# A two-block network on one core: five edits to the order of work in the second mixer

## The chip, the core and the metric

The kernel runs on one core of a Trainium2 chip. The metric is device time in microseconds (us) of one execution. TensorE (PE) multiplies and transposes, ScalarE (ACT) applies functions and copies, VectorE (DVE) does element-wise arithmetic, SyncE (SP) issues the DMA of the weight stream, GpSimd (POOL) does a little at the start and the end.

## The reference

256 tokens of width 2048 pass through two blocks, and all of it is fp32.

- Block one: RMS norm, an input projection, a pooling mixer, a sparse attention with three branches, gates, and an output projection, added to x.
- Block two, where the change lies: `h = rmsnorm(x)`, `z = h @ w_in`. z is split into q, k, v and a forget gate of 8 attention heads of 128 (forgetting attention), and into q, k, v, input gate, forget gate and output gate `mo` of 4 cell heads (mLSTM; q and k 128 wide, v 256 wide; two chunks of 128 tokens). Then

```
cell  = sigmoid(mo) * cell
mixed = concat(head_rmsnorm(att), head_rmsnorm(cell))
x     = x + mixed @ w_out
x     = x + peer_ffn(rmsnorm(x))        # 8 heads, 128x128 experts
out   = rmsnorm(x)
```

head_rmsnorm divides each head (128 or 256 wide) by its own root mean square over its elements, plus 1e-6 under the root.

## The kernel before, in words

**The weight stream.** All weights arrive as 484 slots of 1 MB (128x2048 fp32). For each slot SP loads one of two raw buffers, ACT rounds it to `whi` (L1011, "the rounding"), DVE subtracts to get the rest `wlo` (L1629, "the rest"), and PE multiplies both halves with both halves of the activations, so that fp32 accuracy is kept. Slots alternate between two buffers. ACT may round slot n+2 when PE has finished slot n (`slot_used`), PE may start slot n when its rest is there (`raw_free`). Each engine works through its own program in the order written; semaphores are the only link between engines. No planner is in play, the order is by hand.

**The second mixer.** Beside the stream slots of the projection, numbered 0 to 23 here (list `MIX`: 8 of `in2_m`, then 16 of `in2_n`, in groups of four, each group filling banks 0 and 1 of PSUM), the attention and the cell are computed in small units. Units of attention u = 0 to 15 stand beside slots 2 to 17; units of the cell u = 0 to 7 stand beside numbers 18 to 25, of which 24 and 25 have no slot: there PE turns (transposes) the mixed activations for the output projection instead.

- On PE a unit turns its probabilities, makes the scores of the unit after the next, runs its slot, and then multiplies probabilities with values (`m_values`). The cell's first four units also make the state.
- On ACT a unit rounds slot n+1 (`mix_split(n+1)`), evacuates the banks if slot n-1 closed a group (`mix_evac(n-1)`: L1305, L1308, or for the last two groups, the output gate `mo`, two Tanh of half the argument at L1311), copies probabilities (`fox_copy`, `m_copy` L1369) and takes exponentials (`fox_exp`, `m_exps` L1361).
- On DVE a cell unit makes the next unit's mask and maximum and weighs its scores (`m_mask`, `m_weigh`), takes the rest of slot n+1, and normalizes its output (`m_out`, L2067 to L2078).
- PE waits for both banks of a group (`bank_free`) before the first slot of the next: slots 8, 12, 16, 20.

**The head norms.** For the attention heads DVE forms the mean square (L2126) in cell unit 1, ACT takes the root (L1391) in the same unit, DVE inverts it (L2129) and scales the heads (L2132) in units 2 and 3. For the cell, `sigmoid_rest` (L2085) makes the sigmoid of Tanh's output, `gate_cells` (L2091) multiplies with it, ACT squares each head (L1375) and takes the second root (L1404), and DVE scales (L2150, two operations).

**The turning.** The mixed activations are 8 pieces. PE turns a piece (L463, 4 transposes), ACT rounds it into hTh (`high_parts`, L1037), DVE takes its rest (`low_parts`, L1619). Pieces 0 to 3 (attention) are turned in cell units 6 and 7; pieces 4 to 7 (cell) need both operations of L2150 and are turned inside the output projection `out2`.

**The output projection.** Its slots are called output slots 0, 1, 2, ... here; 16 in all (L580). Output slot 0 needs pieces 0 and 1 of hTh and hTl and waits for pieces up to 3; output slot 2 needs pieces 4 and on. The function `mixed` (L896) turns pieces 4 to 7 ahead of output slot 2.

Of the kernel before, what the change touches and what calls it, by code (L numbers as in the profile page):

```python
# [28 lines left out]
ALU = mybir.AluOpType  # L29
# [132 lines left out]
def build_two_blocks(nc, x, stream, cmpw, params, stage1, mixw_in, fnw1, fnw, gates_dram, out):  # L162
# [6 lines left out]
    with ExitStack() as ctx:  # L169
# [32 lines left out]
        def region(a, n):  # L202
            return R[:, a:a + n]
# [92 lines left out]
        roots = st[:, 260:264]  # L296
        scales = st[:, 264:268]
        one = st[:, 300:302]
        weighted = region(0, TB * D).rearrange("p (b d) -> p b d", b=TB)
        unused3 = region(TB * D, TB * D).rearrange("p (j c) -> p j c", j=8)  # L300
        part_sq = st[:, 232:240]
# [150 lines left out]
        def _(pe):  # L452
# [443 lines left out]
            def mixed(i, h, s):  # L896
                if (h, s) == (0, 0):
                    pe.wait_ge(hTl_part, 16 + 4)
                if (h, s) == (0, 2):
                    for f in range(4, 8):  # L900
                        turn_piece(2, f)
                if h == 0 and s >= 2:
                    pe.wait_ge(hTl_part, 16 + 2 * (s + 1))
# [96 lines left out]
        def _(act):  # L1000
# [290 lines left out]
            def mix_split(n):  # L1291

                if n < len(MIX):
                    split(*MIX[n])
                elif n == len(MIX):
                    split("out2", 0, 0)
# [45 lines left out]
            fox_exp(0)  # L1342
            mix_split(MIX_FIRST)
            for u in range(units):
                mix_split(u + MIX_FIRST + 1)
                mix_evac(u + MIX_FIRST - 1)
                fox_copy(u)
                if u + 1 < units:
                    fox_exp(u + 1)
                if u == CONV_UNIT + 8:  # L1350
                    act.wait_ge(conv_done, 8)
                    A(conv, conv, ACT.Silu).then_inc(conv_silu, 1)
                if u >= 2:
                    fox_square(u - 2)
# [26 lines left out]
            fox_square(FH * TB - 1)  # L1381
            for u in range(units):
                n = MIX_FIRST + FH * TB + u
                mix_split(n + 1)
                mix_evac(n - 1)
                if u + 1 < units:
                    m_exps(u + 1)
                m_copy(u)
                if u == 1:
                    act.wait_ge(head_ms, 1)  # L1390
                    A(hrt[:, :, 0:8], hss[:, :, 0:8], ACT.Sqrt).then_inc(head_rt, 1)  # L1391
                if u == 4:
                    cell_square(0, 0)
                    cell_square(0, 1)
                if u == 6:
                    cell_square(1, 0)
                    cell_square(1, 1)
                if u >= 6:
                    high_parts(2, "mixnorm", range(2 * (u - 6), 2 * (u - 6) + 2))
# [161 lines left out]
        @block.gpsimd  # L1561
        def _(pool):
            step = stepper(pool, pool_step)
            bufs = pool_buf
            inv = s1("invcnt").rearrange("p (g t) -> p g t", g=NG)
            nc.gpsimd.memset(one, 1.0).then_inc(one_set, 1)
            pool.wait_ge(stage1_in, 16)
            for b in range(2):
                pool.wait_ge(bank_free[b], B0["in_u"][b] + 2)
            step(nc.gpsimd.memset(region(pool_at, 2 * W), 0.0))  # L1570
            for c in range(2 * NG):
                g, w = c // 2, WINDOWS[c // 2]
                u = pT[:, U0 + c, :]
                step(nc.gpsimd.tensor_copy(bufs[0][:, PAD:], u))
                a, s = 0, 1
                while s < w:

                    step(nc.gpsimd.tensor_tensor(bufs[1 - a][:, PAD:], bufs[a][:, PAD:], bufs[a][:, PAD - s:PAD - s + T],
                                                 ALU.add))
                    a, s = 1 - a, 2 * s  # L1580

                step(nc.gpsimd.tensor_scalar(bufs[1 - a][:, PAD:], bufs[a][:, PAD:], 1.0 / w, None, ALU.mult))
                step(nc.gpsimd.tensor_tensor(bufs[1 - a][:, PAD:PAD + 16], bufs[a][:, PAD:PAD + 16], inv[:, g, :],
                                             ALU.mult))
                nc.gpsimd.tensor_tensor(u, bufs[1 - a][:, PAD:], u, ALU.subtract).then_inc(pooled, 1)
                pool.wait_ge(pooled, c + 1)

            pool.wait_ge(fnw_in, 16)
            for c in range(4):
                cs = slice(c * 512, (c + 1) * 512)  # L1590
                pool.wait_ge(x3_ready, c + 1)
                nc.gpsimd.tensor_tensor(weighted[:, 0, cs], xres[:, 0, cs], raw[0][:, cs], ALU.mult).then_inc(x3_weighted[0], 1)
# [3 lines left out]
        def _(dve):  # L1596
# [368 lines left out]
            def mix_split(n):  # L1965

                if n < len(MIX):
                    split(*MIX[n])
                elif n == len(MIX):
                    split("out2", 0, 0)  # L1970
# [90 lines left out]
            def m_out(u):  # L2061
                c, h = divmod(u, MH)
                a = u % 2
                dve.wait_ge(m_num, u + 1)
                dve.wait_ge(m_sm, u + 1)
                if c == 1:
                    step(V.tensor_scalar(numt[:, a, :], bank[2 + a][:, MV:2 * MV], mst[:, a, 4:5], None, ALU.mult))  # L2067
                    V.scalar_tensor_tensor(out=mst[:, a, 5:6], in0=bank[6 + a][:, P:P + 1], scalar=mst[:, a, 4:5],
                                           in1=mst[:, a, 5:6], op0=ALU.mult, op1=ALU.add)
                    step(V.tensor_tensor(numt[:, a, :], bank[2 + a][:, 0:MV], numt[:, a, :], ALU.add))  # L2070
                else:
                    step(V.tensor_copy(numt[:, a, :], bank[2 + a][:, 0:MV]))

                step(V.tensor_scalar(mst[:, a, 6:7], mst[:, a, 5:6], -1.0, None, ALU.mult))
                step(V.tensor_tensor(mst[:, a, 6:7], mst[:, a, 6:7], mst[:, a, 5:6], ALU.max))
                step(V.tensor_tensor(mst[:, a, 6:7], mst[:, a, 6:7], mst[:, a, 3:4], ALU.max))
                step(V.reciprocal(mst[:, a, 7:8], mst[:, a, 6:7]))
                V.tensor_scalar(scr2[:, c, 1024 + h * MV:1024 + (h + 1) * MV], numt[:, a, :], mst[:, a, 7:8], None,  # L2078
                                ALU.mult).then_inc(m_read, 1)

            def sigmoid_rest(g):

                for b in range(TB):
                    dve.wait_ge(bank_free[b], B0["in2_n"][b] + 3 + g)
                step(V.tensor_scalar(vN2[:, 4 + g], vN2[:, 4 + g], 0.5, 0.5, ALU.mult, ALU.add))  # L2085

            def gate_cells(c, h, n):

                dve.wait_ge(m_read, MH * c + h + n)
                sl = scr2[:, c, 1024 + h * MV:1024 + (h + n) * MV]  # L2090
                V.tensor_tensor(sl, sl, vN2[:, 4 + h // 2, c, h % 2 * MV:(h % 2 + n) * MV], ALU.mult).then_inc(cells, 1)  # L2091

            def m_scaled(h):

# [15 lines left out]
            for u in range(units):  # L2110
                n = MIX_FIRST + FH * TB + u
                mix_evac(n - 1)
                if u + 1 < units:
                    m_mask(u + 1)
                    m_weigh(u + 1)
                if u + 1 < MH:
                    m_scaled(u + 1)
                if u < MH:
                    m_state(u)
                mix_split(n + 1)  # L2120
                if u >= 6:
                    low_parts(2, "mixnorm", range(2 * (u - 6), 2 * (u - 6) + 2))
                m_out(u)
                if u == 1:
                    dve.wait_ge(head_sq, FH * TB)
                    V.tensor_scalar(hss[:, :, 0:8], hss[:, :, 0:8], 1.0 / DH, EPS, ALU.mult, ALU.add).then_inc(head_ms, 1)  # L2126
                if u == 2:
                    dve.wait_ge(head_rt, 1)
                    step(V.reciprocal(hrt[:, :, 0:8], hrt[:, :, 0:8]))  # L2129
                if u in (2, 3):  # L2130
                    fa = scr2[:, u - 2, 0:1024].rearrange("p (h e) -> p h e", h=FH)
                    V.tensor_tensor(fa, fa, bc(hrt[:, u - 2, 0:8].unsqueeze(2), [P, FH, DH]), ALU.mult).then_inc(xn_ready, 1)  # L2132
                if u == 3:
                    sigmoid_rest(0)
                    gate_cells(0, 0, 2)
                if u in (4, 5):
                    gate_cells(1, u - 4, 1)
                if u == 6:
                    sigmoid_rest(1)
                    gate_cells(0, 2, 2)  # L2140
                if u in (6, 7):
                    gate_cells(1, u - 4, 1)

            dve.wait_ge(head_sq, FH * TB + units)
            V.tensor_scalar(hss[:, :, 8:12], hss[:, :, 8:12], 1.0 / MV, EPS, ALU.mult, ALU.add).then_inc(head_ms, 1)
# [346 lines left out]
```

## Time and profile before

| what | value |
|---|---|
| three timed runs | 3084.39, 3084.81, 3084.92 us, median 3084.81 |
| the profiled execution, time | 3083.82 us |
| its span, first to last instruction | 3082.0 us |
| mean granted clock of TensorE | 0.990 |
| busy share of the span | PE 97%, weight loads 87%, DVE 57%, ACT 41%, POOL 1% |
| chain that ended last | PE 83%, DVE 11%, ACT 4% |
| slots 0 to 23 of the second mixer | about 1140 to 1330 us of the span |
| output projection `out2` | from 1344.5 us of the span |

The profile is of one execution. Times in the views are counted from the start of the span. The time in brackets at the end of a row of the timeline is the idle time of that engine just ahead of it, and who ended it. The profiled execution's own time is 1.8 us over its span.

### The profile page before, as it was taken

The page shows a single profiled execution, that of the slowest core. Times are in us where ns is not written, and L with a number is a line of the kernel's source. Part 1 is how long each engine was busy: PE and PEld are TensorE (multiplying, and loading weights), DVE is VectorE, ACT ScalarE, POOL GpSimd, SP SyncE. Part 2 cuts the span into 40 slices and gives each one's busy share as a digit, 9 for nine tenths or more (in the row PEclk, how much of TensorE's full clock was granted, in tenths as well). Part 3 has the DMA queues.
Part 4 walks back from the last instruction along what each step waited for, and adds up shares of the span by engine and source line. Part 5 has one row for each costly group of instructions (what it writes and reads, how often), then busy time and mean ns, then how long its engine had stood idle before and what let it go on. Part 6 is the DMA issues. An engine that isn't in the chain of part 4 may idle for free.

```text
span 3082.0 us, 46953 instructions
## 1 busy us (share of the span) xinstructions
PE 2984.3 (97%) x18947; PEld 2689.7 (87%) x18947; DVE 1750.0 (57%) x2414; ACT 1253.0 (41%) x1491; POOL 44.8 (1%) x62
## 2 busy tenths in 40 slices
PE   8999999999998999889999999999999999999998
PEld 7887899999987888767899999988888999988887
DVE  5555555554555556565589988744445454444444
ACT  4334444544344334444343344444443333334444
POOL 0000022000000000000000000000000000000000
PEclk9999999999999999989999999999999999999999
DMA  5555433335444554334544455455556655545554
GB/s 206 203 202 222 175 139 119 129 137 177 178 174 153 190 184 146 123 107 160 185 163 176 160 171 174 166 189 192 191 195 232 242 186 178 185 178 195 191 191 177
DMA packets 90195, 542.56 MB, mean 176 GB/s; under 512 B 9328, under 2 KB 25840, under 8 KB 26352
## 3 DMA queue, kind: packets, MB, share of 16 engines
q1 hardware_dynamic: 70992, 513.94, 46.8%
q10 hardware_dynamic: 19104, 27.27, 2.5%
q8 instruction: 67, 1.10, 0.1%
q14 instruction: 32, 0.26, 0.0%
HBM read 530.68 MB, written 10.49 MB: 176 GB/s over the span
## 4 chain that ended last, share of the span: by engine, by line
PE 83%; DVE 11%; ACT 4%; issue 1%; DMA 0%; ACTq 0%; DVEq 0%; SPq 0%
PE bank L487 28%; PE bank L961 23%; PE bank L500 9%; PE bank L580 8%; PE bank L504 5%; DVE wlo L1629 4%; PE bank L555 3%; ACT whi L1011 2%; PE bank L753 2%; PE bank L620 1%; DVE R L2255 1%; PE bank L710 1%; DVE hT L1619 1%; DVE R L2250 1%; DVE R L2263 0%
## 5 line engine op out<-in xcount | busy, mean ns | idle before, releaser
L1629 DVE TENSOR_TENSOR wlo<-raw,whi 128x2048 fp32r<-128x2048 f32 (+1 forms) x484 | 1103.7, 2281 | 1135.5 <-ACT whi L1011 1134.2
L1011 ACT ACTIVATE whi<-raw 128x2048 fp32r<-128x2048 f32 (+1 forms) x484 | 920.9, 1903 | 1318.7 <-PE bank L961 411.4
L487 PE MATMUL bank<-hT,whi 128*128 128x256 f32 x6400 | 1192.8, 287 | 6.6 <-DVE wlo L1629 5.0
L487 PEld LDWEIGHTS bank<-hT,whi 128*128 128x128 f32 x6400 | 993.9, 192 | 11.4 <-DVE wlo L1629 5.4
L487 PE MATMUL bank<-hT,wlo 128*128 128x256 f32 x3200 | 904.5, 283 | 0.0
L487 PEld LDWEIGHTS bank<-hT,wlo 128*128 128x128 f32 x3200 | 611.7, 191 | 0.0
L500 PE MATMUL bank<-hT,whi 128*128 128x512 f32 x1280 | 447.7, 399 | 3.0 <-DVE wlo L1629 3.0
L504 PE MATMUL bank<-hT,wlo 128*128 128x256 f32 x1280 | 343.9, 281 | 1.3 <-DVE wlo L1629 1.3
L500 PEld LDWEIGHTS bank<-hT,whi 128*128 128x128 f32 x1280 | 236.2, 188 | 58.5 <-issue 6.6
L961 PE MATMUL bank<-whi,ghi 128*128 128x512 f32 x1016 | 273.3, 391 | 6.1 <-DVE glo L2327 6.1
L961 PE MATMUL bank<-wlo,ghi 128*128 128x512 f32 x1016 | 272.8, 391 | 0.0
L961 PE MATMUL bank<-whi,glo 128*128 128x512 f32 x1016 | 271.7, 389 | 0.0
L580 PE MATMUL bank<-whi,hT 128*128 128x512 f32 x768 | 242.9, 395 | 15.5 <-DVE wlo L1629 9.9
L504 PEld LDWEIGHTS bank<-hT,wlo 128*128 128x128 f32 x1280 | 240.7, 189 | 7.8 <-DVE wlo L1629 1.7
L961 PEld LDWEIGHTS bank<-whi,ghi 128*128 128x128 f32 x1016 | 191.4, 189 | 46.1 <-issue 6.5
L961 PEld LDWEIGHTS bank<-wlo,ghi 128*128 128x128 f32 x1016 | 191.8, 189 | 40.1
L961 PEld LDWEIGHTS bank<-whi,glo 128*128 128x128 f32 x1016 | 190.9, 188 | 39.8
L580 PEld LDWEIGHTS bank<-whi,hT 128*128 128x128 f32 x768 | 146.2, 190 | 50.1 <-issue 18.2
L580 PE MATMUL bank<-wlo,hT 128*128 128x512 f32 x384 | 151.1, 394 | 0.0
L945 PE MATMUL bank<-R 128*128 128x128 f32 x512 | 98.9, 274 | 2.5 <-DVE R L2255 2.2
L555 PE MATMUL bank<-whi,hT 128*128 128x512 f32 x256 | 87.5, 414 | 9.7 <-ACT R L1311 4.9
L580 PEld LDWEIGHTS bank<-wlo,hT 128*128 128x128 f32 x384 | 73.3, 191 | 15.0
(322 smaller groups left out, 1976.5 us busy)
## 6 DMA issues: line engine op xcount, KB each, us to landing
raw<-stream SPq DMA_DIRECT2D x484, 1024.0 KB, 4.8
R<-cmpw ACTq DMA_DIRECT2D x8, 1024.0 KB, 5.6
gates_dram<-R ACTq DMA_DIRECT2D x64, 128.0 KB, 4.7
R<-gates_dram ACTq DMA_DIRECT2D x16, 512.0 KB, 5.1
xres<-x SPq DMA_DIRECT2D x2, 1024.0 KB, 5.9
R<-mixw ACTq DMA_DIRECT2D x1, 1024.0 KB, 6.6
R<-fnw ACTq DMA_DIRECT2D x1, 1024.0 KB, 6.3
raw<-fnw SPq DMA_DIRECT2D x1, 1024.0 KB, 4.7
```

The lines of the kernel that those rows point to most:

```text
L487: last = mm(bank[b][:, t * T:(t + 1) * T], w[t][:, ks], x_[:, k, :], start=(at == 0 and n == 0), stop=(at == KC - 1 and n == 2))
L500: return mm(bank[s][:], whi[t][:, k * P:(k + 1) * P], hT2[:, k, :, :].rearrange("p a t -> p (a t)"), start=(k == 0), stop=(k == KC - 1))
L504: mm(bank[s][:, 0:T], wlo[t][:, k * P:(k + 1) * P], hTh[:, k, :], start=False, stop=False)
L555: last = mm(bank[b][:], x_[:, k, ts_], w[t][:, kk * 512:(kk + 1) * 512], start=(k == 0 and n == 0), stop=(k == KC - 1 and n == 2))
L580: last = mm(bank[2 * h + b][:], x_[:, k, ts_], w[t][:, kk * 512:(kk + 1) * 512], start=(k == 0 and n == 0), stop=(k == KC - 1 and n == 2))
L620: last = mm(bank[6 + v][0:NC4, 0:CH], kb[v][:, l, :], cw[n % 2][:, ll * CH:(ll + 1) * CH], start=(l == 0), stop=(l == CB - 1))
L710: last = mm(o, vN1[:, br, k, kv * DH:(kv + 1) * DH], PT[:, a, j * P:(j + 1) * P], start=False, stop=(j == 2 * nb - 1))
L753: last = mm(bank[s][:, e * T:(e + 1) * T], w[t][:, ks], y[:, k, :], start=(k == 0 and m == 0), stop=(k == 7 and m == 2))
L945: last = mm(bank[4 + (2 * s + q) % 4][:, c * P:(c + 1) * P], second_hot[:, k // 2, :], first_hot[:, k // 2, :], start=True, stop=True)
L961: last = mm(bank[4 * b + c][:], x_[:, t, ts_], w[t][:, c * 512:(c + 1) * 512], start=(first and s == 0 and n == 0), stop=(last_group and s ...
L1011: A(whi[t][:, 0:w], raw[t][:, 0:w], ACT.Copy).then_inc(hi_ready[t], 1)
L1629: V.tensor_tensor(wlo[t][:, 0:w], raw[t][:, 0:w], whi[t][:, 0:w].bitcast(F32), ALU.subtract).then_inc(raw_free[t], 1)
```

## The change

Five edits, all in block two's mixer.

1. ACT: `mix_evac(n-1)` stands ahead of `mix_split(n+1)`, in the attention units and in the cell units.
2. ACT: the root of the attention heads' mean square moves from cell unit 1 to cell unit 0, and a dummy Exp follows it (on two constants of a new pair `back`). DVE forms the mean square in unit 0, between the rest of slot 19 and `m_out(0)`.
3. ACT: in cell units 6 and 7 `m_copy(u)` stands ahead of `m_exps(u+1)`.
4. DVE: `m_out` multiplies with 0.5 in its last operation, and the gate is (Tanh + 1) times that in one operation: `sigmoid_rest`'s operation (two of them, L2085) is gone, its waits stay (`tanh_made`). The gates of heads 2 (both chunks) and 3 (chunk 0) move from the end of unit 6 to unit 7, behind the rests of pieces 2 and 3 and ahead of `m_out(7)`.
5. PE: pieces 4 to 7 are turned ahead of output slot 1 instead of output slot 2.

```diff
+        back = st[:, 302:304]
...
-                if (h, s) == (0, 2):
+                if (h, s) == (0, 1):
                     for f in range(4, 8):
                         turn_piece(2, f)
...
             for u in range(units):
+                mix_evac(u + MIX_FIRST - 1)
                 mix_split(u + MIX_FIRST + 1)
-                mix_evac(u + MIX_FIRST - 1)
                 fox_copy(u)
...
                 n = MIX_FIRST + FH * TB + u
+                mix_evac(n - 1)
                 mix_split(n + 1)
-                mix_evac(n - 1)
+                if u >= units - 2:
+                    m_copy(u)
                 if u + 1 < units:
                     m_exps(u + 1)
-                m_copy(u)
-                if u == 1:
+                if u < units - 2:
+                    m_copy(u)
+                if u == 0:
                     act.wait_ge(head_ms, 1)
                     A(hrt[:, :, 0:8], hss[:, :, 0:8], ACT.Sqrt).then_inc(head_rt, 1)
+                    A(back[:, 1:2], back[:, 0:1], ACT.Exp)
...
-            nc.gpsimd.memset(one, 1.0).then_inc(one_set, 1)
+            nc.gpsimd.memset(st[:, 300:304], 1.0).then_inc(one_set, 1)
...
-                V.tensor_scalar(scr2[:, c, 1024 + h * MV:1024 + (h + 1) * MV], numt[:, a, :], mst[:, a, 7:8], None,
-                                ALU.mult).then_inc(m_read, 1)
+                V.tensor_scalar(scr2[:, c, 1024 + h * MV:1024 + (h + 1) * MV], numt[:, a, :], mst[:, a, 7:8], 0.5,
+                                ALU.mult, ALU.mult).then_inc(m_read, 1)
...
-                step(V.tensor_scalar(vN2[:, 4 + g], vN2[:, 4 + g], 0.5, 0.5, ALU.mult, ALU.add))
...
-                V.tensor_tensor(sl, sl, vN2[:, 4 + h // 2, c, h % 2 * MV:(h % 2 + n) * MV], ALU.mult).then_inc(cells, 1)
+                V.scalar_tensor_tensor(out=sl, in0=vN2[:, 4 + h // 2, c, h % 2 * MV:(h % 2 + n) * MV], scalar=1.0, in1=sl,
+                                       op0=ALU.add, op1=ALU.mult).then_inc(cells, 1)
...
                 mix_split(n + 1)
+                if u == 0:
+                    dve.wait_ge(head_sq, FH * TB)
+                    V.tensor_scalar(hss[:, :, 0:8], hss[:, :, 0:8], 1.0 / DH, EPS, ALU.mult, ALU.add).then_inc(head_ms, 1)
                 if u >= 6:
                     low_parts(2, "mixnorm", range(2 * (u - 6), 2 * (u - 6) + 2))
+                if u == 7:
+                    gate_cells(0, 2, 2)
+                    gate_cells(1, 2, 1)
                 m_out(u)
-                if u == 1:
-                    dve.wait_ge(head_sq, FH * TB)
-                    V.tensor_scalar(hss[:, :, 0:8], hss[:, :, 0:8], 1.0 / DH, EPS, ALU.mult, ALU.add).then_inc(head_ms, 1)
...
                 if u == 3:
-                    sigmoid_rest(0)
+                    tanh_made(0)
                     gate_cells(0, 0, 2)
                 if u in (4, 5):
                     gate_cells(1, u - 4, 1)
                 if u == 6:
-                    sigmoid_rest(1)
-                    gate_cells(0, 2, 2)
-                if u in (6, 7):
-                    gate_cells(1, u - 4, 1)
+                    tanh_made(1)
+                if u == 7:
+                    gate_cells(1, 3, 1)
```

## Rows read from the trace of the kernel before

**Rows 1.** The profile's page, busy time by engine and share of the span.

```profile
PE 2984.3 (97%) x18947; PEld 2689.7 (87%) x18947; DVE 1750.0 (57%) x2414; ACT 1253.0 (41%) x1491; POOL 44.8 (1%) x62
```

**Rows 2.** Windows: stretch, length, busy by engine, clock, DMA share, GB/s.

```profile
1259.00:1310.00 51.00, 43.92 (x175) 34.86 (x176) 23.77 (x67) 19.33 (x36) 0.00 (x0) 0.87 0.29 103
```

**Rows 3.** Waits, 1139 to 1420: engine, line, releaser: us, times, longest.

```profile
PE bank L555 <- ACT R L1311: 4.9, 1, 4.9
...
PE bank L580 <- DVE wlo L1629: 6.9, 2, 6.0
...
PE bank L580 <- DVE hT L1619: 2.4, 1, 2.4
```

**Rows 4.** Timeline of PE: first matmul of slots 8, 12 and 16.

```profile
1200.40 0.47 PE L555 MATMUL bank<-whi,hT 128*128 128x512 f32 x1 [1.40 <-issue]
...
1229.80 0.50 PE L555 MATMUL bank<-whi,hT 128*128 128x512 f32 x1 [1.35 <-ACT R L1308]
...
1259.20 0.50 PE L555 MATMUL bank<-whi,hT 128*128 128x512 f32 x1 [1.99 <-ACT R L1308]
```

**Rows 5.** Chain of waits: start, us, what; slots 15, 16 and 20.

```profile
1251.01 5.66 PE bank L555 x24
...
1259.20 7.37 PE bank L555 x24
...
1301.16 7.19 PE bank L555 x24
```

**Rows 6.** Timeline of ACT, the evacuation ahead of slot 12.

```profile
1229.17 0.58 ACT L1308 ACTIVATE R<-bank 128x512 f32<-128x512 f32 x1
```

**Rows 7.** Timeline of ACT, cell units 1 and 2.

```profile
1287.32 1.91 ACT L1011 ACTIVATE whi<-raw 128x2048 fp32r<-128x2048 f32 x1 [8.12 <-PE bank L555]
...
1291.02 1.28 ACT L1391 ACT_TABLE_LOAD   x1
1296.64 0.22 ACT L1391 ACTIVATE st<-st 128x16 f32<-128x16 f32 x1 [4.34 <-DVE st L2126]
...
1298.68 1.28 ACT L1311 ACT_TABLE_LOAD   x1
1299.97 1.08 ACT L1311 ACTIVATE R<-bank 128x512 f32<-128x512 f32 x2
```

**Rows 8.** Timeline and source line: last table load ahead of block one's Tanh.

```profile
379.04 1.28 ACT L1164 ACT_TABLE_LOAD   x1
...
L1183 ACT ACTIVATE R<-bank,par x32: 448/451/476, 525.3 to 747.3; 128x256 f32<-128x256 f32 x32
```

**Rows 9.** Chain of waits, first and last row of a stretch of DVE.

```profile
1308.81 0.44 DVE R L2072
...
1322.11 2.21 DVE wlo L1629
```

**Rows 10.** Timeline of DVE, end of the cell.

```profile
1340.94 0.69 DVE L2085 TENSOR_SCALAR R<-R 128x1024 f32<-128x1024 f32 x1
1341.66 1.03 DVE L2091 TENSOR_TENSOR R<-R 128x512 f32<-128x512 f32 x2
...
1350.40 2.28 DVE L1629 TENSOR_TENSOR wlo<-raw,whi 128x2048 fp32r<-128x2048 f32 x1
```

**Rows 11.** Timelines of PE, ACT and DVE around output slots 1 to 3.

```profile
1358.33 1.91 PE L463 MATMUL bank<-par,R 128*128 128x128 f32 x16
...
1358.97 3.03 ACT L1037 ACTIVATE hT<-bank,par 128x256 fp32r<-128x256 f32 x8 [9.31 <-PE bank L463]
...
1359.85 3.23 DVE L1619 SCALAR_TENSOR_TENSOR hT<-bank,par,hT 128x256 fp32r<-128x256 f32 x8 [7.16 <-ACT hT L1037]
...
1361.83 3.76 ACT L1011 ACTIVATE whi<-raw 128x2048 fp32r<-128x2048 f32 x2
1373.45 1.92 ACT L1011 ACTIVATE whi<-raw 128x2048 fp32r<-128x2048 f32 x1 [7.86 <-PE bank L580]
1378.89 1.92 ACT L1011 ACTIVATE whi<-raw 128x2048 fp32r<-128x2048 f32 x1 [3.52 <-PE bank L580]
```

More of the change, by code:

```diff
@@ L2077, in m_out, with tanh_made @@
                 step(V.reciprocal(mst[:, a, 7:8], mst[:, a, 6:7]))
-                V.tensor_scalar(scr2[:, c, 1024 + h * MV:1024 + (h + 1) * MV], numt[:, a, :], mst[:, a, 7:8], None,
-                                ALU.mult).then_inc(m_read, 1)
-            def sigmoid_rest(g):
+                V.tensor_scalar(scr2[:, c, 1024 + h * MV:1024 + (h + 1) * MV], numt[:, a, :], mst[:, a, 7:8], 0.5,
+                                ALU.mult, ALU.mult).then_inc(m_read, 1)
+            def tanh_made(g):
                 for b in range(TB):
                     dve.wait_ge(bank_free[b], B0["in2_n"][b] + 3 + g)
-                step(V.tensor_scalar(vN2[:, 4 + g], vN2[:, 4 + g], 0.5, 0.5, ALU.mult, ALU.add))
             def gate_cells(c, h, n):
```

## The prediction

> **What bounds the kernel now.** I read the busy shares first: TensorE is busy 97% of the span [rows 1], so only what PE waits for, or runs at the low clock, can be won. The windows over the second mixer then show where that is: in the stretch of the cell units PE is busy 43.9 of 51 us at a mean granted clock of 0.87 [rows 2], while the whole span has 0.99. Third, the waits of that stretch name three places [rows 3]: PE waits 4.9 us for ScalarE's Tanh ahead of slot 20, up to 6.0 us for VectorE's rest ahead of output slot 2, and 2.4 us for hTl ahead of output slot 0. The timeline adds three small ones, 1.40, 1.35 and 1.99 us ahead of slots 8, 12 and 16 [rows 4]. After the longer ones the next slot is slow: slot 15 took 5.66 us, slots 16 and 20, after gaps, 7.37 and 7.19 [rows 5]; that is the 1.2 GHz level for their first part, 2.4 GHz after. The gaps ahead of slots 8 and 12 have no slow slot behind them.
>
> **Edit 1, evacuation first.** ACT rounds slot n+2 (1.91 us, the operation as in [rows 7]) and only then evacuates for 0.58 us [rows 6]; both wait for the same last matmul. Turned round, the bank is free 0.58 us after the slot, when PE is still in the small matmuls between two slots. At slots 8 and 12 these take longer than 0.58 us, so the idle time goes whole: 1.40 + 1.35. Ahead of slot 16 there are no scores to make (the units end) and some 0.25 us stay: 1.99 − 0.25 = 1.75. Sum 4.5 us. With that gap no larger than the small ones, slot 16 should run at the full clock: 7.37 − 5.66 = 1.7 us more. The price: the rounding comes 0.6 us later at these places. It is hidden, since rounding and rest together take 1.91 + 2.3 us and PE's slot over 5.6 us; probabilities and exponentials behind the pair on ACT keep their time, as the pair's sum is the same.
>
> **Edit 2, the root in unit 0.** Before, ACT loads the root's table at 1291.02, waits for VectorE's mean square until 1296.64 (4.34 us), then rounds slot 21, loads a table for Tanh (1.28) and does two Tanh in 1.08 [rows 7]. All of that stood between slot 19 and slot 20. In unit 0 ACT is idle 8.12 us until the rounding at 1287.32 [rows 7]; the new work there is load 1.28, a wait for DVE's mean square (behind the rest of slot 19, about 1282.5), the root 0.2, load 1.28, the dummy Exp: about 5 us, done near 1284.2, and covered. VectorE's new wait in unit 0 is for squares made some 6 us earlier, and what is queued behind it is `m_out(0)`, which waits for PE until 1287 anyway. So neither costs anything; without the cover each would cost its own length once.
> At unit 2 two Tanh now follow slot 19 directly: 1.08 us, against the about 1.6 us of small matmuls that PE has there. The 4.9 us go whole, and the slow part of slot 20 with them, 7.19 − 5.66 = 1.5. Sum 6.4. Late next is VectorE. From `m_out(2)` at 1308.81 to the rest of slot 23 at 1324.3 the chain is VectorE's alone [rows 9]: 15.5 us for two units, and PE's own work for the same was 16.2, so it just fits; one `sigmoid_rest` operation less (0.69, [rows 10]) makes it 14.8. For slots 21 and 22 I get margins of 2 and 0.6 us in the same way. So the gain is kept up to slot 23.
> That Tanh needs no load behind an Exp is shown in block one: the last load ahead of its Tanhs (525 to 747 us) is an Exp's, at 379.04, and the next is a Silu's at 671 [rows 8]. If it needed one here, 1.28 us come in front, of which PE would feel some 0.8.
>
> **Edit 3, copy first in units 6 and 7.** PE's `m_values(6)` starts earlier, but the chain at the end goes through masks, exponentials and pieces, not through it. What remains is one copy less (about 0.15 us) ahead of the rounding of pieces 0 and 1.
>
> **Edit 4, gates.** Between `m_out(6)` and the rests of pieces 2 and 3 VectorE had 0.69 us of `sigmoid_rest` and 1.03 us of gates [rows 10], 1.67 from start to start. The first is gone, the second stands behind the rests. The rests are ready by then: PE turns piece 2 as soon as the rest of piece 0 exists, as before. Output slot 0 so starts 1.67 + 0.15 = 1.8 us sooner. The end of the cell (roots, L2150) comes sooner only by what is really removed: 0.72 + 0.15 = 0.87. The gate's operation with two steps costs as much as with one (the rests, of the same kind with three operands, take 0.40 each in [rows 11], a gate of the same 256 columns 0.43), and the extra factor 0.5 in `m_out` I take at 0, bounded by 0.1 us in each of eight.
>
> **Edit 5, turning ahead of output slot 1.** Before: VectorE's rest for output slot 1 ends at 1350.40 + 2.28 = 1352.7 [rows 10]; slot 1 runs until 1358.3; then 16 transposes 1.91, ACT's eight parts 3.03 and two roundings 3.76, VectorE's eight parts 3.23 and the rest of slot 2 [rows 11], and PE stands idle for 6.0 us [rows 3]. From start of slot 1 to start of slot 2: 13.5 us. After, counted from the start t of VectorE's rest for slot 1: PE turns from about t + 0.3 (slot 0 ends there, and the last L2150 has just ended) to t + 2.3; the rest is there at t + 2.3; slot 1 runs to t + 8.0. ACT rounds the pieces from t + 0.9 to 3.9, then slot 2 to 5.8. VectorE takes the pieces' rests from t + 2.3 to 5.5 and slot 2's from 5.8 to 8.0. So slot 2 starts at t + 8.1, 5.8 after slot 1. The gain is 13.5 − 5.8 = 7.7, with the 0.87 above 8.6. Three chains meet here within 0.2 us (turns against the rest of slot 1, VectorE against slot 1 itself), so this is the softest term; whichever is late costs its lateness. Output slot 2 also loses its slow part: it ended at 1373.45, 7.15 us after its start at 1366.3, the next took 5.44 [rows 11]: 1.7. From there PE runs without a gap in either case. The stream does not bind: raw buffers are freed some 5.9 us before they are wanted at the tightest place.
>
> **The sum.** 4.5 + 1.7 + 6.4 + 8.6 + 1.7 = 22.9 us, of 3083.82 of the profiled execution: 3060.9. The median of the runs lies 0.99 above that execution, so 3061.9, and I say 3062.0.
>
> **A rule weighed.** The low level follows the gap of 1.99 us but not those of 1.40 and 1.35 [rows 4, 5]. The Trainium skill ("TensorE: Matmul & The Clock Gate", the section on the HAM clock gate) says that the low clock is the default, released by activity, and that the moment of change is not tied to the kernel's work and shifts between runs. By the rows alone three slow parts go (1.7 + 1.5 + 1.7 = 4.9 us); by the rule such parts may turn up at other places. It is the first rival.
>
> **The rivals.**
> - *The clock falls elsewhere.* The gaps close but the three slow parts come back behind the low activity that stays (between attention and cell, and in units 6 and 7). Gain 22.9 − 4.9 = 18: 3067. For it: the mean clock of 0.87 over a stretch with few long gaps [rows 2]. Against: in the rows each slow part stands right behind a gap that goes. 12%.
> - *The turn is given back.* The transposes run at the low clock (1.9 us more, in front of slot 1), or VectorE, with 7.8 us of work in a row and no rest between, holds slot 2 up by 2 to 3 us, which brings back a slow part too. Gain 17 to 19: 3067. For it: three chains within 0.2 us. Against: output slot 0 runs just ahead of the turns for 7 us, the last part at the full clock. 13%.
> - *The tail's gap stays whole*, because something I do not see holds the turns: gain 12.6, 3072. 5%.
> - *Nothing arrives.* A later stage takes the time up. Against it: PE-bound, back to back for some 80 us behind output slot 2. About 3085. 4%.
> - *Slower: PE at the low level for whole slots.* With the turns and the second rounding pressed into output slots 0 and 1 PE waits in short pieces, and the clock does not come back. A slot at 1.2 GHz costs 5.66 us more. From four such slots (22.6) on the whole gain is used up; six give 3096. Against: no slot in the rows is slow for its whole length. 3%.
>
> **How the numbers follow.** My forecast of 3062 has 63%, its own band 3058.5 to 3065.5 (0.1 in each `m_out`, the Tanh's load of 0.8, the soft term). With the first two rivals 88% lie under 3069; I give 3057.5 to 3069.0. Under 0.2% (6 us) a measurement of this kernel would hardly tell a change from none. Faster by more than that: 63 + 12 + 13 + 5 = 93%; within: 4%; slower: 3%.
>
> **What would show it.** The slots 8, 12 and 16 start with under 0.3 us of idle time; slot 20 starts right behind its small matmuls and takes 5.7 us; L1391 has no wait ahead of a rounding, and Tanh no load; output slot 0 starts 14.6 − 1.8 = 12.7 us after slot 23 ends and output slot 2 27.8 us after it (36.3 before). The forecast is wrong if PE has a gap of over 1 us ahead of slot 20 or output slot 2, or if the granted clock over the cell units stays at 0.87 while the gaps are gone.

## The result, and the profile after

| | before | after |
|---|---|---|
| median of the runs | 3084.86 us | 3062.20 us |
| the profiled execution | 3083.82 us | 3062.96 us |
| its span | 3082.0 us | 3061.2 us |
| mean granted clock | 0.990 | 0.992 |
| slot 7's end to slot 23's end | 132.3 us | 118.9 us |
| slot 23's end to output slot 2's end | 43.5 us | 33.5 us |

The ratio is 0.9923 (95% interval 0.9906 to 0.994): 23.8 us faster by the ratio, 22.7 by the medians. The forecast was 3062.0. The two last lines of the table are taken from the timelines (start of the small matmuls behind slots 7 and 23, start of the rounding that waits for output slot 2). They give 13.4 + 10.0 = 23.4 us inside the stretch that was changed. The spans differ by 20.8 only, since slot 7 ended 2.8 us later in the profile after, 1200.4 against 1197.65, in stages that the change does not touch; 2.6 us of it are longer busy time of PE for the same matmuls, so low clock. Behind output slot 2 both profiles take the same time to the end, 1708.6 and 1708.3 us: no later stage took the gain back.

The busy time of PE, on the page of the changed kernel [rows 1]: 5.4 us less over the whole span, at the same number of matmuls.

```profile
PE 2978.9 (97%) x18947; PEld 2686.7 (88%) x18947; DVE 1748.6 (57%) x2412; ACT 1253.5 (41%) x1492; POOL 44.8 (1%) x62
```

Windows over the stretch that was changed, first of the kernel before, then of the changed kernel [rows 2]: slot 7's end to slot 23's end, and slot 23's end to output slot 2's end. The clock is the third column from the end.

```profile
1197.65:1329.96 132.31, 120.59 (x531) 96.29 (x530) 84.73 (x195) 55.42 (x104) 0.00 (x0) 0.95 0.35 124
1329.96:1373.45 43.49, 30.88 (x127) 24.46 (x126) 26.55 (x60) 17.77 (x40) 0.00 (x0) 0.80 0.27 97
```

```profile
1200.44:1319.38 118.94, 116.67 (x532) 93.87 (x531) 84.77 (x194) 55.85 (x105) 0.00 (x0) 0.97 0.39 137
1319.38:1352.87 33.49, 26.94 (x127) 21.33 (x126) 25.38 (x59) 18.01 (x41) 0.00 (x0) 0.95 0.28 96
```

PE is busy for 143.6 us there instead of 151.5, and idle for 8.8 instead of 24.3. So of the 23.4 us some 7.9 are clock and 15.5 idle time. Over the matmuls of the window in [rows 2], from slot 16 to slot 20 (174 of its 175), the clock went from 0.87 to 0.92:

```profile
1257.46:1299.40 41.94, 39.94 (x174) 32.23 (x175) 25.13 (x70) 20.88 (x37) 0.00 (x0) 0.92 0.32 110
```

Waits of PE in the changed kernel, 1139 to 1400 [rows 3]. The three long ones are gone; what is left lies in the tail, between slot 23 and output slot 1, but for 1.43 us of the first line, which stand ahead of slot 18 and stood there before too:

```profile
PE bank L853 <- DVE st L2063: 3.8, 2, 2.4
...
PE bank L464 <- DVE hT L1624: 1.8, 1, 1.8
...
PE bank L464 <- DVE R L2157: 1.3, 1, 1.3
...
PE bank L581 <- DVE hT L1624: 0.8, 1, 0.8
```

First matmul of slot 16 in PE's timeline [rows 4], with 0.28 us of idle time in place of 1.99. Slots 8 and 12 have none at all.

```profile
1257.46 0.47 PE L556 MATMUL bank<-whi,hT 128*128 128x512 f32 x1 [0.28 <-ACT R L1309]
```

Slots 16 and 20 in the chain of waits [rows 5], 5.73 and 5.44 us instead of 7.37 and 7.19. (Without a gap ahead of it the first matmul of slot 20 starts while the small ones still run, and the chain leaves these 0.35 us out: in the timeline the slot lasts from 1292.17 to 1297.96, 5.8 us.)

```profile
1257.46 5.73 PE bank L556 x24
...
1292.52 5.44 PE bank L556 x24
```

ScalarE in cell units 0 to 2 of the changed kernel [rows 7]. Root and both loads stand between 1275.8 and 1280.9, all in its idle time (2.63 us of it are left in front of the rounding). The two Tanh follow slot 19 without a load, and the rounding of slot 21 comes behind them:

```profile
1275.84 1.28 ACT L1395 ACT_TABLE_LOAD   x1
1279.20 0.21 ACT L1395 ACTIVATE st<-st 128x16 f32<-128x16 f32 x1 [2.08 <-DVE st L2128]
1279.43 1.28 ACT L1396 ACT_TABLE_LOAD   x1
1280.73 0.20 ACT L1396 ACTIVATE st<-st 128x1 f32<-128x1 f32 x1
1283.56 1.91 ACT L1012 ACTIVATE whi<-raw 128x2048 fp32r<-128x2048 f32 x1 [2.63 <-PE bank L556]
...
1290.75 1.08 ACT L1312 ACTIVATE R<-bank 128x512 f32<-128x512 f32 x2 [3.51 <-PE bank L556]
1291.72 1.92 ACT L1012 ACTIVATE whi<-raw 128x2048 fp32r<-128x2048 f32 x1
```

The tail on PE: the end of slot 23 (L862), output slot 0, the turning, output slot 1:

```profile
1319.38 0.60 PE L862 MATMUL bank<-R 128*128 128x256 f32 x2
...
1332.09 0.47 PE L581 MATMUL bank<-whi,hT 128*128 128x512 f32 x1 [0.85 <-DVE hT L1624]
...
1339.05 1.97 PE L464 MATMUL bank<-par,R 128*128 128x128 f32 x16 [1.27 <-DVE R L2157]
1341.25 0.50 PE L581 MATMUL bank<-whi,hT 128*128 128x512 f32 x1 [0.23 <-DVE wlo L1634]
```

and on VectorE [rows 10, 11]: the rests of slot 1, of the pieces and of slot 2 follow each other, with 0.28 us between the last two.

```profile
1338.91 2.29 DVE L1634 TENSOR_TENSOR wlo<-raw,whi 128x2048 fp32r<-128x2048 f32 x1
1341.11 3.22 DVE L1624 SCALAR_TENSOR_TENSOR hT<-bank,par,hT 128x256 fp32r<-128x256 f32 x8
1344.61 2.29 DVE L1634 TENSOR_TENSOR wlo<-raw,whi 128x2048 fp32r<-128x2048 f32 x1 [0.28 <-ACT whi L1012]
```

Output slot 2 follows slot 1 without a gap: PE goes on at 1347.0, where slot 1 ends. ScalarE's roundings behind slot 1 and slot 2 show it [rows 11]:

```profile
1347.12 1.92 ACT L1012 ACTIVATE whi<-raw 128x2048 fp32r<-128x2048 f32 x1 [2.55 <-PE bank L581]
1352.87 1.92 ACT L1012 ACTIVATE whi<-raw 128x2048 fp32r<-128x2048 f32 x1 [3.83 <-PE bank L581]
```

### The profile page after: what moved, and what is told of

Same layout as the page of the kernel before. It is cut to its first block, busy times and chain, and to the rows that moved or that the text cites. A ratio compares the mean times of both kernels' runs of the same rounds, so it can differ in the third digit from the quotient of the medians.

```text
span 3061.2 us, 46950 instructions
## 1 busy us (share of the span) xinstructions
PE 2978.9 (97%) x18947; PEld 2686.7 (88%) x18947; DVE 1748.6 (57%) x2412; ACT 1253.5 (41%) x1492; POOL 44.8 (1%) x62
## 4 chain that ended last, share of the span: by engine, by line
PE 84%; DVE 10%; ACT 4%; issue 1%; DMA 0%; ACTq 0%; DVEq 0%; SPq 0%
PE bank L488 29%; PE bank L962 23%; PE bank L501 9%; PE bank L581 8%; PE bank L505 5%; DVE wlo L1634 4%; PE bank L556 3%; ACT whi L1012 2%; PE bank L754 2%; PE bank L621 1%; DVE R L2262 1%; PE bank L711 1%; DVE hT L1624 1%; DVE R L2257 1%; DVE R L2270 0%
```

## The experiments

The theory is the prediction's list of steps, with one addition made for the runs: edits 1 and 2 meet at slot 20 and are not independent there. The rivals are in the expectations. Two measures are given for each run: the ratio to the kernel before with its 95% interval, from repeated runs of both kernels on the same chip; and stretches inside the profile, from which low-clock parts of other stages are kept out. The intervals are 5 to 8 us wide, so single microseconds rest on the stretches alone. "Stretch 1" is slot 7's end to slot 23's end (132.3 us before, 118.9 after), "stretch 2" slot 23's end to output slot 2's end (43.5 and 33.5).

### Edit 1 alone

```diff
-                mix_split(u + MIX_FIRST + 1)
                 mix_evac(u + MIX_FIRST - 1)
+                mix_split(u + MIX_FIRST + 1)
```

and the same for `n` in the cell units.

> Edit 1 alone on the kernel before: the evacuation ahead of the rounding, in the attention and the cell units. Theory A (my steps, which interact at slot 20): slots 8, 12, 16 give 4.5 us, slot 16's slow part 1.7; and at slot 20, with the root still in unit 1, the banks come free after wait, table load and two Tanh, without the rounding of 1.9 us between: 1.9 more. Sum 8.1 us, 3076.7. Theory B (the edits are independent and slot 20 belongs to edit 2): 6.2 us, 3078.6. Theory C (the evacuation only shifts the wait to the later rounding): 0 to 2 us. In the trace: idle ahead of slots 8, 12, 16 under 0.3 us and slot 20 about 3 us behind its small matmuls under A, 4.9 under B.

Ratio 0.9975 (0.9966 to 0.9983), 7.7 us (5.2 to 10.5), which allows A and B and rules out C. The stretch decides: 124.2 us, 8.1 less than before, as A has it. First matmul of slot 20 in this kernel's timeline of PE:

```profile
1294.38 0.47 PE L555 MATMUL bank<-whi,hT 128*128 128x512 f32 x1 [3.08 <-ACT R L1311]
```

3.08 us of idle time instead of 4.88: edit 1 alone takes 1.8 us of a wait that the change's title gives to the root.

### Edit 2 alone

```diff
-                if u == 1:
+                if u == 0:
                     act.wait_ge(head_ms, 1)
                     A(hrt[:, :, 0:8], hss[:, :, 0:8], ACT.Sqrt).then_inc(head_rt, 1)
+                    A(back[:, 1:2], back[:, 0:1], ACT.Exp)
```

with VectorE's mean square moved likewise.

> Edit 2 alone: root of the attention heads in unit 0, dummy Exp behind it, order of rounding and evacuation as before. Theory A: behind slot 19 ScalarE still rounds 1.82 us and then does two Tanh (1.08), the banks are free 2.9 us after the slot, PE's small matmuls take 1.6 to 1.9: 1.3 us of idle time stay of 4.9. Gain 3.6, and the slow part of slot 20 (1.5) goes too, as gaps of 1.4 had none behind them: 5.1 us, 3079.8. Theory B (independent edits): 6.4 us, 3078.4. Theory C (the table loads and the new wait in unit 0 cost what they save): within 1 us of before.

Ratio 0.9989 (0.998 to 0.9998), 3.4 us (0.6 to 6.2). Stretch 1: 128.8, 3.5 less. The idle time ahead of slot 20 is 1.27 us, as A has it, but the slow part of slot 20 stays. PE's timeline of this kernel and its window over slot 20:

```profile
1297.69 0.57 PE L556 MATMUL bank<-whi,hT 128*128 128x512 f32 x1 [1.27 <-ACT R L1312]
```

```profile
1297.70:1304.80 7.10, 7.10 (x24) 5.75 (x25) 3.16 (x6) 0.66 (x3) 0.00 (x0) 0.76 0.40 147
```

The slot took 7.1 us at a mean clock of 0.76, behind a gap shorter than the 1.40 and 1.35 us that slots 8 and 12 had without harm [rows 4]. So A's size of the gap is right and its 1.5 us for the clock is not. The measured 3.5 is the 3.6 of the gap alone. The ratio's interval would allow all of A and the upper end of C; only B lies outside it, and barely. The stretch decides.

### Edits 1 and 2 together

> Edits 1 and 2 together. The steps of the prediction: 4.5 + 1.7 + 6.4 = 12.6 us, 3072.2, with no idle time over 0.3 us ahead of slots 8, 12, 16, 20 and slot 20 in 5.7 us or less. Under theory A of the two single runs the sum of the singles (8.1 + 5.1 = 13.2) is about what both give; the wait at slot 20 is split between them. If the cell units are bound by VectorE once the gap is gone, slots 21 to 23 show waits for its rest and the sum is 2 to 3 us smaller.

Ratio 0.9964 (0.9951 to 0.9977), 11.1 us (7.1 to 15.1). Stretch 1: 119.2 us, 13.1 less. Slots 8, 12 and 20 have no idle time ahead of them, slot 16 has 0.27, and slot 20 takes 5.6 us. The singles sum to 8.1 + 3.5 = 11.6; the rest, 1.5, is the slow part of slot 20, which neither edit removes alone. The third possibility did not occur: of slots 21 to 23 only slot 23 has to wait for VectorE's rest (ready at 1312.26, slot 23 starts at 1312.31), and that by about 0.2 us, as in the kernel before.

### Edit 5 alone

```diff
-                if (h, s) == (0, 2):
+                if (h, s) == (0, 1):
```

> Edit 5 alone: pieces 4 to 7 turned ahead of output slot 1. My steps: in the kernel before output slot 0 ends at 1351.7 and the rest of slot 1 is there at 1352.7, so the turning (1.9 us) ends 0.9 us too late and holds slot 1 by that; gain 7.7 - 0.9 + slow part of output slot 2 (1.7) = 8.5 us, 3076.4. Rival: the turning ahead of slot 1 is only worth it with the gates moved; alone slot 1 is held by 2 us or more and VectorE holds slot 2: gain 5 or less, 3080.

Ratio 0.9979 (0.997 to 0.9988), 6.5 us (3.7 to 9.3). Stretch 2: 35.5 us, 8.0 less than before, against 8.5 expected. The turning starts when output slot 0 ends, at 1351.98, and slot 1 follows it at 1353.6, 23.4 us behind slot 23 where it was 22.8 before (0.9 later was expected, 0.6 it is); slot 2 waits 0.57 us for VectorE. The stretch rules the rival (5 us or less) out; the timing alone would allow it.

### The changed kernel without edit 5

> The changed kernel without edit 5: pieces 4 to 7 turned ahead of output slot 2 again. My steps: output slots 0 and 1 as in the changed kernel (slot 1 starts 11.5 us sooner than before), then 1.9 us of turning and 6.0 us of idle time ahead of slot 2, and its slow part. Slower than the changed kernel by 7.7 + 1.4 = 9.1 us: 3071.3. Rival (the turn is hidden already by the gates moved in edit 4): by under 4 us.

Ratio 0.9971 (0.9959 to 0.9983). Stretch 2: 45.3 us, 11.8 longer than in the changed kernel, where 9.1 was expected. First matmuls of output slots 1 and 2 in its timeline of PE:

```profile
1339.73 0.80 PE L581 MATMUL bank<-whi,hT 128*128 128x512 f32 x1 [3.44 <-DVE wlo L1634]
...
1354.85 0.77 PE L581 MATMUL bank<-whi,hT 128*128 128x512 f32 x1 [6.02 <-DVE wlo L1634]
```

The rival is ruled out. What I had not counted: output slot 0 now ends 3.4 us ahead of slot 1's rest, and without the turning in that time PE idles and runs slot 1 at the low clock too (the turning starts at 1346.9, 7.2 us after slot 1). The turning fills this hole, and that is worth 1.4 us beside its own. A further 1.0 us is clock in output slot 2: it takes 8.3 us here (1354.85 to 1363.16, mean granted clock 0.68), where I had put the 7.2 of the kernel before.

### The changed kernel without edit 4

```diff
+                step(V.tensor_scalar(vN2[:, 4 + g], vN2[:, 4 + g], 0.5, 0.5, ALU.mult, ALU.add))
...
                 if u == 6:
                     tanh_made(1)
+                    gate_cells(0, 2, 2)
+                if u in (6, 7):
+                    gate_cells(1, u - 4, 1)
```

with the gates of unit 7 and the factor 0.5 taken out.

> The changed kernel without edit 4: the sigmoid's operations back, the gates at the end of unit 6, no factor in m_out. Output slot 0 starts 1.7 us later and the chain of the cell ends 0.7 us later. Theory A: output slot 0 runs at the full clock (5.7 us) as in the changed kernel, ends ahead of the turning's release, and only 0.7 us are lost: 3062.9. Theory B: its clock is low again (7.2 us, as in the kernel before and in the runs of edits 1 and 2 alone), it ends after the release and the turning comes behind the rest of slot 1: 1.5 to 2 us lost, 3064.

Ratio 0.9934 (0.9921 to 0.9948). Stretch 2: 35.3 us, 1.8 more, which is B. Output slot 0, the turning, slots 1 and 2 in its timeline of PE:

```profile
1333.99 0.47 PE L581 MATMUL bank<-whi,hT 128*128 128x512 f32 x1 [2.48 <-DVE hT L1624]
...
1341.16 1.91 PE L464 MATMUL bank<-par,R 128*128 128x128 f32 x16
...
1342.83 0.48 PE L581 MATMUL bank<-whi,hT 128*128 128x512 f32 x1
...
1349.11 0.47 PE L581 MATMUL bank<-whi,hT 128*128 128x512 f32 x1 [0.56 <-DVE wlo L1634]
```

Slot 0 starts 14.4 us behind slot 23 (12.7 in the changed kernel), takes 7.2 us and so ends at 1341.16, behind the release of the turning at 1339.95. The turning then holds slot 1, by 0.6 us over its rest, which is ready at 1342.15. The run takes back both halves of edit 4, the removed operation and the moved gates; which of them slot 0's clock hangs on was not run.

### The changed kernel without edit 3

> The changed kernel without edit 3: in units 6 and 7 the copy behind the exponentials again. My step: 0.15 us later at output slots 0, 1 and 2, which no timing shows: 3062.3. Rival: m_values(6) and m_values(7) then come late on PE, in front of output slot 0, and cost the 1 us that they take: 3063.3.

Ratio 0.9925 (0.9912 to 0.9939). Stretch 2: 33.7 us, 0.2 more. `m_values(6)` again has 3.3 us of idle time ahead of it, and nothing that ends the stage waits for it. Output slot 0 starts 12.9 us behind slot 23 where the changed kernel has 12.7 in both of its profiles. The step is right, its size too small for a timing. (This kernel's median lies 2.9 us over the changed kernel's beside it, and its profiled execution as much. Of that, 1.5 us stand ahead of slot 8, which started at 1201.9, and 1.5 us behind output slot 2; the edit touches neither.)

### The changed kernel without the dummy Exp

> The changed kernel without the dummy Exp behind the root. Theory A: the next function that needs the table is the exponential of unit 1, not Tanh, so the load of 1.28 us stands in unit 1 ahead of it, in time in which ScalarE waits for VectorE's maximum (1.1 us); at most 0.2 us of it is late there, PE feels nothing: 3062.2. Theory B, as the prediction has it for a Tanh that needs a load: the 1.28 us stand between slot 19 and slot 20, of which PE feels 0.8: 3063.0.

Ratio 0.9924 (0.991 to 0.9937). ScalarE's timeline of this kernel:

```profile
1283.06 1.28 ACT L1362 ACT_TABLE_LOAD   x1
1284.35 0.40 ACT L1362 ACTIVATE R<-R,st 128x128 f32<-128x128 f32 x1
...
1288.31 1.08 ACT L1312 ACTIVATE R<-bank 128x512 f32<-128x512 f32 x2 [3.31 <-PE bank L556]
```

The load stands ahead of unit 1's exponential, directly behind a rounding, and Tanh waits 3.3 us for PE as before. Stretch 2 is 33.5 us and PE has no gap from slot 18 to slot 23. The Exp is worth nothing here.

### The changed kernel once more

> The changed kernel once more, unchanged, for the clock. Output slot 0 took 5.7 us (full clock) in its profile and 7.2 in five of the others. Theory A: the moment at which the clock comes back is not tied to the program; in this profile slot 0 can be of either length, the time is 3062.2 within 1.5 us, and the stretches ahead of the change (block one) differ by a slow part or two between two profiles of one program. Theory B: the program's order sets it; slot 0 takes 5.7 us again, and slot 8 starts at 1201.8 us again within 0.3.

Ratio 0.9919 (0.9906 to 0.9933), median 3062.05. Slot 8 started at 1200.46 instead of 1201.8; the stages ahead are the same program, so a low-clock part moves by 1.3 us between two executions, as A says. But output slot 0 ran at the full clock again, as B says:

```profile
1331.05 0.47 PE L581 MATMUL bank<-whi,hT 128*128 128x512 f32 x1 [0.77 <-DVE hT L1624]
```

The turning behind it again waited 1.27 us for VectorE. Neither theory holds as a whole. (Slot 0 was slow in seven of the nine other profiles that there were before this run, not in five.) The stretches repeat well: 119.2 and 33.5 us here, 118.9 and 33.5 in the first profile.

### Two further versions

First: pieces 0 and 1 rounded ahead of the last exponentials.

```diff
                 if u >= units - 2:
                     m_copy(u)
+                if u == 6:
+                    high_parts(2, "mixnorm", range(0, 2))
                 if u + 1 < units:
                     m_exps(u + 1)
...
-                if u >= 6:
-                    high_parts(2, "mixnorm", range(2 * (u - 6), 2 * (u - 6) + 2))
+                if u == 7:
+                    high_parts(2, "mixnorm", range(2, 4))
```

> The changed kernel with one more move: in unit 6 ScalarE rounds pieces 0 and 1 ahead of the exponentials of unit 7, in the 3.4 us in which it waits for VectorE's maximum. VectorE then takes their rests directly behind weighing unit 7, 1.2 us sooner, and all behind it moves: output slot 0, the cell's root, output slots 1 and 2 by 1.2 us. 3061.0. Rival: the exponentials come late by the four parts and the chain loses what it gains: within 0.3 us of the changed kernel.

Ratio 0.9925 (0.9912 to 0.9939). Output slots 0, 1 and 2 in its timeline of PE (slot 23 ended at 1320.92):

```profile
1332.33 0.47 PE L581 MATMUL bank<-whi,hT 128*128 128x512 f32 x1 [2.17 <-DVE hT L1626]
...
1341.49 0.50 PE L581 MATMUL bank<-whi,hT 128*128 128x512 f32 x1
...
1347.42 0.47 PE L581 MATMUL bank<-whi,hT 128*128 128x512 f32 x1 [0.20 <-DVE wlo L1636]
```

Slot 0 starts 11.4 us behind slot 23 instead of 12.7. It runs at the low clock, 7.2 us, and yet slot 1 starts 1.3 sooner, since it has to wait for its rest anyway. Stretch 2 is 32.3 us, 1.2 less, as expected.

Second, on top: slot 1's rest in VectorE's idle time, slot 2's ahead of the pieces, the turning in the middle of slot 1.

```diff
+                            if midway is not None and (h, s, kk) == (0, 1, 1):
+                                midway()
...
-            for c, h in ((0, 2), (0, 3), (1, 2), (1, 3)):
+            for c, h in ((0, 2), (0, 3), (1, 2)):
                 cell_square(c, h)
+            split("out2", 0, 1)
+            cell_square(1, 3)
...
-            split("out2", 0, 1)
+            split("out2", 0, 2)
             high_parts(2, "mixnorm", range(4, 8))
```

> On top of the last run (pieces 0 and 1 rounded ahead of the last exponentials): the rest of output slot 1 is taken while VectorE waits for the last square and root, slot 2 is rounded and its rest taken ahead of pieces 4 to 7, and these pieces are turned in the middle of output slot 1, behind its 12th matmul. Output slot 1 then follows slot 0 directly and slot 2 follows slot 1. Theory A, with output slot 0 at the full clock: output slot 2 starts 2.7 us sooner after slot 23 than in the changed kernel (24.9 instead of 27.6 us): 3059.4. With slot 0 at the low clock 1.5 us of it are lost. Rival: VectorE's 2.2 us for the rest of slot 1 push the cell's scaling back and PE waits in the middle of slot 1 by as much: within 0.5 us of the last run.

Ratio 0.9918 (0.9904 to 0.9931). Output slot 0 and the turning inside slot 1 in its timeline of PE (slot 23 ended at 1319.36):

```profile
1330.77 0.77 PE L581 MATMUL bank<-whi,hT 128*128 128x512 f32 x1 [1.11 <-DVE hT L1631]
...
1340.66 1.91 PE L464 MATMUL bank<-par,R 128*128 128x128 f32 x16
...
1342.32 0.48 PE L581 MATMUL bank<-whi,hT 128*128 128x512 f32 x1
```

Slot 0 was slow (the other half of the expectation), slot 2 starts at 1345.4, 26.0 us behind slot 23 instead of 27.7. The turning has no idle time ahead of it, so the wait in the middle of slot 1 that the rival names did not come. Stretch 2 is 31.5 us, 2.0 less than in the changed kernel and 0.8 less than in the last run. In time both versions are the same as the changed kernel within what the timings can tell (0.9918 for the second against 0.9919 for the changed kernel on one chip). That they are faster is shown in the profiles, each of one execution, and by no timing.

## Why the prediction was right

| term | predicted | in the profiles |
|---|---|---|
| idle time ahead of slots 8, 12, 16 | 4.5 | 1.40 + 1.35 + 1.71 = 4.5 |
| slow part of slot 16 | 1.7 | 1.6 |
| slot 20, gap | 4.9 | 4.9 |
| slot 20, slow part | 1.5 | 1.75 by the chain of waits, 1.4 by the timeline |
| output slot 0 sooner after slot 23 (not in the sum) | 1.8 | 14.56 − 12.71 = 1.85 |
| output slot 2 sooner after slot 23 | 8.6 | 36.3 − 27.7 = 8.6 |
| slow part of output slot 2 | 1.7 | 1.4 |
| sum | 22.9 | 22.7 by the terms, 23.4 by the stretches |

**What bounds it.** Right: all that was won was idle time of PE and its low clock. The stretches give 0.7 us more than the terms; about half of it is slot 18, which was 0.4 us shorter by clock (7.05 against 7.42 in the chain of waits), a thing the edits do not touch. Another 0.2 is slot 23: before, it started when VectorE's rest was ready (1324.32, slot 23 at 1324.37). From slot 22's end to slot 23's end it is 7.64 to 7.69 us in the six profiles without edit 4 and 7.48 or 7.49 in the seven with it. Part of the close hit is luck: the median came within 0.2 us of the forecast while the terms and the stretches differ by 0.7 and stages that nobody changed move single executions by more than that.

**Edit 1.** Right in size and place, 0.28 us left at slot 16 where I had 0.25. What the prediction did not say, and the single run shows, is that this edit also carries 1.8 us of slot 20's wait. Its reading of slot 16 was off in one point: the slot began at full clock and fell to the low level 0.6 us in, as the windows of the kernel before show, 0.88 for its first microsecond and 0.50 for its second.

```profile
1259.20:1260.20 1.00, 0.99 (x4) 0.86 (x5) 1.00 (x1) 0.98 (x2) 0.00 (x0) 0.88 0.00 0
1260.20:1261.20 1.00, 1.00 (x4) 0.80 (x3) 1.00 (x2) 0.99 (x4) 0.00 (x0) 0.50 0.00 0
```

**Edit 2.** The gap is right. The prediction put all of ScalarE's load and wait between slots 19 and 20; but slot 19 ended at 1294.3, so the load (from 1291.02) and half of the wait lay ahead of that, and only the last 2.3 us up to 1296.64 stood behind it. The account of the parts was silent on one thing: moved alone, the root would have won 3.5 us, since the rounding would have stood where the root had stood. The "late next" was right: PE had no wait for VectorE's rest from slot 21 to slot 23 in the changed kernel. The prediction's case of a load ahead of Tanh cannot arise even without the Exp: the load goes to whichever function needs it first, and that is unit 1's exponential, with time to spare.

**Edit 3.** 0.15 us predicted, 0.2 measured with the edit undone.

**Edit 4.** The start of output slot 0 and the cell's end came sooner as worked out (slot 1 starts 21.9 us behind slot 23, the prediction's figures give 21.9). But I had slot 0 at the low clock, ending just as the turning is released, and it ran at the full clock in 5.7 us. So the turning waited 1.27 us for the cell's scaling (L2157, L2150 before) where I had none. It did not move the sum: the turning hung on the scaling instead, which ended within 0.3 us of where I had put the end of slot 0, and the chains met as worked out. The turning ended at 1341.02 and the rest of slot 1 at 1341.20; VectorE's rest of slot 2 at 1346.90 and slot 1 at 1347.0. That the wrong clock of slot 0 cost nothing is partly luck. Other runs show the other case: with slot 0 slow the turning only just fits (1341.40 against 1341.44 in the first further version) or is late by 0.6 (without edit 4). The factor and the second step of the gate cost nothing, as assumed: the last operation of `m_out` takes 0.35 us with and without the factor, two gates 1.02 against 1.03.

**Edit 5.** The term that I called the softest held to 0.1 us. The rival that the turn is given back did not come: the 16 transposes took 1.97 us against 1.91 before, and VectorE was done 0.1 us ahead of PE.

**The rival of the clock** was half there. The Trainium skill ("TensorE: Matmul & The Clock Gate", the section on the HAM clock gate) has it that the moment of change shifts between runs: the two profiles of the changed kernel agree with it, by 1.3 us ahead of slot 8 and by 0.2 us at slot 18. But the slow parts that I named went in both and did not come back elsewhere in the stretch, so the 4.9 us of that rival were kept. What stays slow is slot 18, behind the gap of 1.43 us that no edit touches: 7.05 and 7.28 us in the two profiles, 7.42 before. The prediction did not list it.

## What to carry to other kernels

When two engines' work hangs on one event, put first what the bounding engine waits for, and count an edit's gain at each place where a second edit removes part of the same wait: alone they won 8.1 and 3.5 us, together 13.1, and what neither reached alone was the clock. Before pricing a moved step, ask which of its parts stand between release and the next use (here 0.58 against 1.91 us), and write the chains that meet at the next wait side by side; the smallest margin tells whether the term is soft. In a long kernel read the gain off a stretch of the profile between two fixed points; the timing of the whole carries up to 4 us from stages that nobody changed (slot 7 ended between 1197.6 and 1201.7 us in the thirteen profiles).

## What the runs showed of the hardware that I had not expected

- The low clock follows not the length of the last gap alone. In the stream of full slots gaps of 1.40 and 1.35 us were followed by a slot at full clock, one of 1.99 by a slow one [rows 4, 5]; in the cell units 1.27 us were followed by a mean clock of 0.76 over slot 20 (edit 2 alone). There PE had run small matmuls for 2.0 us just before, against 1.35 us ahead of slots 8 and 12, and 0.7 ahead of slot 16. What decides is left open.
- Output slot 0 took 5.7 us in the five profiles where PE's idle time just ahead of it was 0.66 to 0.96 us, and 7.2 or more in those where it was 1.1 to 3.3 us. That both profiles of the changed kernel agree speaks for an order that is set by the program here, while ahead of slot 8 it moved. What decides is left open.
- In the cell units each table load started as soon as the operation before it on ScalarE was done, ahead of the wait of the function that needed it (1275.84, three microseconds before the root could run), and it took 1.28 us with no further pause before the next function (1279.43 to 1280.73). A function moved into idle time there brought its load along for nothing. It is no rule for every place: in block one the load of the Silu, at 671.33, came only behind a wait of 1.09 us for PE.
